# Expert stage of a decoder layer: another order of the half-width gating on VectorE and ScalarE

## The chip, the core and the metric

The kernel runs on one NeuronCore of a Trainium2 chip. The metric is the device time of one execution in microseconds, here the median of three: 2575.46 (2571.65 to 2578.45).

The engines: TensorE (PE) multiplies matrices, VectorE (DVE) and ScalarE (ACT) work on tiles element by element, GpSimd (POOL) gathers rows, SyncE (SP) issues the weight transfers. Each runs its own list of instructions in order and waits at semaphores for the others.

## The reference

One decoder layer on 1024 tokens of width 1024: attention and a convolution side by side, a mixture of experts, and a gated per-layer embedding, with RMSNorm between. The change touches the experts alone:

```python
# 1024 tokens, each sent to 4 of 32 experts; rows are grouped by expert
gu   = rows @ w_gate_up[e] + b_gate_up[e]            # 1024 -> 2 * 1024
gate = minimum(gu[:, :D_FF], 7.0)
up   = clip(gu[:, D_FF:], -7.0, 7.0)
hid  = (up + 1.0) * (gate * sigmoid(gate * 1.702))
out  = hid @ w_down[e] + b_down[e]                   # 1024 -> 1024
y    = sum over a token's 4 experts, weighted by its gates
```

## The kernel before

Three stages follow one another: attention and routing (to about 740 us), the experts (to about 2405), and the rest of the layer.

The expert stage works through a list of *items*. An item is up to 128 rows of one expert; where an expert has 1 to 32 rows more than that, the item carries them along as a *tail* in plain fp32. With these inputs there are 38 items, 8 with a tail. An item reads the expert's weights in 12 *pieces* of 1 MB: pieces 0 to 3 are the gate and up columns of the first half of the hidden width (half 0), 4 to 7 those of half 1, 8 to 11 the down projection. A piece passes through four hands:

- SP issues its transfer into one of 6 slots of `raw` as soon as the slot's last piece has been split (L500 to L506, `expert_piece`; in `slot_free` it waits for `lo_ready`);
- ACT rounds it: `whi` = the piece in fp32r (L1734, `split_hi`), 6 slots, up to 6 pieces ahead of PE;
- DVE takes the remainder: `wlo` = `raw` - `whi` (L868, `split_lo`), 4 slots, up to 4 pieces ahead;
- PE multiplies three times for each 128 rows and 512 columns (L609 to L611, `three`): `whi` by the rows' rounded part, `whi` by their remainder, `wlo` by the rounded part. That is 12 matmuls of 512 columns a piece, 144 an item. At the end of each piece it raises `w_free`.

Between the pieces stands the gating, once for each half. When the gate columns of piece 3 (or 7) are through, `gate_done` rises; DVE clamps `gat`, ACT takes the sigmoid of `gat` (L1747), DVE multiplies (L883), clamps `upc` (L887) and forms `hid` (L892). PE transposes `hid` (L596, `turn_hidden`): for half 0 behind piece 5, for half 1 behind piece 8. ACT rounds the transpose (`hhi`, L1751), DVE takes the remainder (`hlo`, L897, `hidden`), and piece 8 needs those of half 0, piece 10 those of half 1. A tail has the same steps on small tiles (`gat_t`, `sig_t`, `hid_t`); PE turns its `hid_t` behind pieces 1 and 5 (L684). Tail products (L668, L676) run four pieces ahead, so an item whose successor has a tail does four of them too.

For the next item, PE turns the gathered rows behind piece 8 (L579), and ACT and DVE split them into `xhi` and `xlo` (L873). At the item's end ACT copies the result to `ysb` (L1767) and writes it out.

The order on each engine is written out by hand: each has a `body` with a loop over c = 0 to 11, one turn a piece. In turn c DVE waits for `w_free` of piece c and then takes the remainder of piece c + 4; ACT waits for the same and rounds piece c + 6. What else an engine does stands in front of or behind that, by the `if` lines. ScalarE's activation functions lie in tables, and the compiler puts an `ACT_TABLE_LOAD` in front of an activation where it can't know that the table is there; at the start of the loop's body it can't.

Of the kernel before, what the change touches and what calls it, by code (L numbers as in the profile page):

```python
# [23 lines left out]
ALU = mybir.AluOpType  # L24
ACT = mybir.ActivationFunctionType
# [17 lines left out]
LIMIT = 7.0  # L43
# [7 lines left out]
PIECES = 12  # L51
# [39 lines left out]
def layer(nc, x, p_in, positions, g_mix_pre, w_in, w_dw, b_dw, g_conv_ln, b_conv_ln, w_out, g_mix_post,  # L91
# [3 lines left out]
    with outer:  # L95
# [5 lines left out]
        def sem(name):  # L101
            return outer.enter_context(nc.semaphore(name))
# [3 lines left out]
        def banks(b, n=1):  # L106
            return bank[:, b:b + n, :].rearrange("p b c -> p (b c)")
# [245 lines left out]
        lo_ready = sem("lo_ready")  # L353
        w_free = sem("w_free")
        gate_done = sem("gate_done")
        gu_used = sem("gu_used")
        gat_ready = sem("gat_ready")
        sig_done = sem("sig_done")
# [198 lines left out]
        def gate_base(half):  # L557
            return 0 if half else 2
# [305 lines left out]
        def experts_dve(dve, finish_gates):  # L864

            def split_lo(n, c):
                dve.wait_ge(hi_ready, PIECES * n + c + 1)
                dve.tensor_tensor(wlo[:, c % LO], raw[:, c % RAW], whi[:, c % HI].bitcast(F32),  # L868
                                  ALU.subtract).then_inc(lo_ready, 1)

            def columns(n):
                dve.wait_ge(xhi_ready, n + 1)
                dve.tensor_tensor(xlo[:].rearrange("p k n -> p (k n)"), banks(XT, 2),  # L873
                                  xhi[:].rearrange("p k n -> p (k n)").bitcast(F32),
                                  ALU.subtract).then_inc(xlo_ready, 1)

            def gate_part(n, half):

                dve.wait_ge(gate_done, 2 * n + half + 1)
                dve.wait_ge(hid_ready, 2 * n + half)  # L880
                dve.tensor_scalar(gat[:], banks(gate_base(half)), LIMIT, None, ALU.min).then_inc(gat_ready, 1)  # L881
                dve.wait_ge(sig_done, 2 * n + half + 1)
                dve.tensor_tensor(sig[:], gat[:], sig[:], ALU.mult).then_inc(gs_done, 1)  # L883

            def up_part(n, half):

                dve.tensor_scalar(upc[:], banks(gate_base(half) + 1), LIMIT, -LIMIT, ALU.min, ALU.max).then_inc(gu_used, 1)  # L887
                dve.wait_ge(gs_done, 2 * n + half + 1)
                dve.wait_ge(gu_used, 2 * n + half + 1)

                dve.wait_ge(ht_done, 2 * n + half)
                dve.scalar_tensor_tensor(out=hid[:], in0=upc[:], scalar=1.0, in1=sig[:],  # L892
                                         op0=ALU.add, op1=ALU.mult).then_inc(hid_ready, 1)

            def hidden(n, half):
                dve.wait_ge(hhi_ready, 2 * n + half + 1)
                dve.tensor_tensor(hlo[:, 4 * half:4 * half + 4].rearrange("p k n -> p (k n)"), banks(HT),  # L897
                                  hhi[:, 4 * half:4 * half + 4].rearrange("p k n -> p (k n)").bitcast(F32),
                                  ALU.subtract).then_inc(hlo_ready, 1)

            def tail_first(k1, half, fetched):

                if half == 0:
                    dve.wait_ge(bias_t_in, 64 * fetched)
                dve.wait_ge(tail_free, PIECES * k1 + 4 * half + 4)
                dve.wait_ge(hid_t_ready, 2 * k1 + half)
                dve.tensor_tensor(sums[:].rearrange("p (g n) -> p g n", g=2),
                                  banks(SUM if half else ACC)[:, 0:256].rearrange("p (g n) -> p g n", g=2),
                                  bias_t[:, :, half], ALU.add).then_inc(sums_ready, 1)
                dve.wait_ge(sums_ready, 2 * k1 + half + 1)  # L910
                dve.tensor_scalar(gat_t[:], sums[:, 0:P], LIMIT, None, ALU.min).then_inc(gat_t_ready, 1)
                dve.tensor_scalar(upc_t[:], sums[:, P:2 * P], LIMIT, -LIMIT, ALU.min, ALU.max).then_inc(upc_t_ready, 1)

            def tail_gated(k1, half):
                dve.wait_ge(sig_t_done, 2 * k1 + half + 1)
                dve.tensor_tensor(sig_t[:], gat_t[:], sig_t[:], ALU.mult).then_inc(gs_t_done, 1)
                dve.wait_ge(gs_t_done, 2 * k1 + half + 1)
                dve.wait_ge(upc_t_ready, 2 * k1 + half + 1)

                dve.wait_ge(htt_done, 2 * k1 + half)  # L920
                dve.scalar_tensor_tensor(out=hid_t[:], in0=upc_t[:], scalar=1.0, in1=sig_t[:],
                                         op0=ALU.add, op1=ALU.mult).then_inc(hid_t_ready, 1)

            def tail_rows(k1, fetched):

                dve.wait_ge(tail_free, PIECES * k1 + PIECES)
                dve.wait_ge(bias_d_in, 64 * fetched)
                dve.wait_ge(ytail_out, 64 * k1)
                dve.tensor_tensor(ysb_t[:], banks(ACC)[:, 0:256], bias_d[:], ALU.add).then_inc(ytail_ready, 1)

            for s in range(2):
                dve.wait_ge(u2_out[s], 16 * NT // 2)
            dve.wait_ge(u2t_done, 2 * NT)
            for c in range(LO):
                split_lo(0, c)
                if c == 1:
                    columns(0)
            dve.wait_ge(stage3_end, 4)
            dve.wait_ge(tab_in, 16)
            items = Items(dve, "dve", (LIVE, TWO), True)  # L940
            with dve.If(items.value(TWO) > 0):
                tail_first(0, 0, 1)
            finish_gates()

            def body(n, k1, tail):
                nk1 = k1 + tail
                for c in range(PIECES):
                    if tail and c == 8:
                        tail_rows(k1, items.kf)
                    if tail and c == 5:  # L950
                        tail_gated(k1, 1)
                    if c in (3, 7):
                        gate_part(n, c // 4)
                        dve.wait_ge(w_free, PIECES * n + c + 1)
                        up_part(n, c // 4)
                    if c == 5:
                        items.ahead(n + 1)
                        nxt, nxt2 = items.value(LIVE), items.value(TWO)
                    if c + LO < PIECES:
                        dve.wait_ge(w_free, PIECES * n + c + 1)  # L960
                        split_lo(n, c + LO)
                    else:
                        with dve.If(nxt > 0):
                            if c == 9:
                                columns(n + 1)
                            dve.wait_ge(w_free, PIECES * n + c + 1)
                            split_lo(n + 1, c + LO - PIECES)
                    if c in (5, 8):
                        hidden(n, c // 8)
                    if tail and c == 0:  # L970
                        tail_gated(k1, 0)
                    if tail and c == 4:
                        tail_first(k1, 1, None)
                    if c == 11:
                        with dve.If(nxt2 > 0):
                            tail_first(nk1, 0, items.kf + tail)

            items.run(body)
            dve.memset(gat[:, 0:1], 0.0).then_inc(stage4_end, 1)
            dve.wait_ge(stage4_end, 4)  # L980
# [597 lines left out]
        def _(act):  # L1578
# [166 lines left out]
            def sigmoid(n, half):  # L1745
                act.wait_ge(gat_ready, 2 * n + half + 1)
                act.activation(sig[:], gat[:], ACT.Sigmoid, scale=ALPHA).then_inc(sig_done, 1)  # L1747
# [44 lines left out]
            def body(n, k1, tail):  # L1792
                nk1 = k1 + tail
                for c in range(PIECES):
                    if tail and c in (2, 6):
                        tail_hidden(k1, c // 4)
                    if c == 7:
                        with act.If(nxt2 > 0):
                            tail_columns(nk1)
                    if c in (3, 7):  # L1800
                        sigmoid(n, c // 4)
                    if tail and c == 5:
                        tail_sigmoid(k1, 1)
                    if c in (5, 8):
# [3 lines left out]
                    if c + HI < PIECES:  # L1808
                        act.wait_ge(w_free, PIECES * n + c + 1)
                        split_hi(n, c + HI)  # L1810
                    else:
                        with act.If(nxt > 0):
                            act.wait_ge(w_free, PIECES * n + c + 1)
                            split_hi(n + 1, c + HI - PIECES)
                            if c == 8:
                                columns(n + 1)
                    if tail and c == 0:
                        tail_sigmoid(k1, 0)
                    if c == 8:
# [457 lines left out]
```

## Time and profile before

| | before |
|---|---|
| median of 3 runs | 2575.46 us (2571.65 to 2578.45) |
| profiled execution | 2574.06 us, span 2572.4 |
| PE busy | 2382.9 us (93% of the span) |
| DVE busy | 1811.8 us (70%) |
| ACT busy | 1444.4 us (56%) |
| POOL busy | 258.8 us (10%) |
| weight remainders (L868) | 456 x 2288 ns |
| weight roundings (L1734) | 456 x 1912 ns |
| table loads | 1283 ns each |
| granted TensorE clock, mean | 0.97 of full |
| DMA | 629.50 MB, mean 245 GB/s over the span |

Busy time says how much an engine did, not whether it set the pace: that is read from the waits of the engine that has least room. A granted clock of 1.00 is 2.4 GHz; the other level is 0.5, 1.2 GHz, so a stretch with a mean of 0.96 spent a part of its time at half speed. A matmul's end is modelled, so successive ones overlap in the rows. In a row of the timeline, the brackets give the idle time of the engine before the instruction and what released it.

### The profile page before, as it was taken

Reading aid. Unit: us, or ns where it says so; the run is one execution under the profiler, and the core shown is the slowest. Engines: PE = TensorE matmul, PEld = TensorE weight load, DVE = VectorE, ACT = ScalarE, POOL = GpSimd, SP = SyncE. Lnnn points to the kernel's source line nnn. Section 1 sums busy time; section 2 is a strip of 40 time slices with the busy share of each in tenths; the row PEclk is TensorE's granted clock in tenths of the full one; section 3 lists DMA queues with packets and bytes.
Section 4 is the critical chain, followed back from the end, with each engine's and each line's share of the span. In section 5 each row is a group of like instructions: output and inputs, shape, how many; then the busy total and the mean of one; then the engine's idle time right before and its main releaser. Section 6 shows DMA issues by size and latency. Waiting matters only on the chain. (4 is left out here: it accounts for less than half of the span.)

```text
span 2572.4 us, 39278 instructions
## 1 busy us (share of the span) xinstructions
PE 2382.9 (93%) x11242; PEld 1587.9 (62%) x11243; DVE 1811.8 (70%) x2101; ACT 1444.4 (56%) x1441; POOL 258.8 (10%) x252
## 2 busy tenths in 40 slices
PE   6999999999869999999999999999999999999898
PEld 3454445545537777677677776777676676776543
DVE  4573555535468888778888787888787787887374
ACT  3113344444346777577767766676665675776344
POOL 1200000001220001000000001000111010011130
PEclk9999999999879999999999999999999999999999
DMA  6007800142358999799999999899988797998651
GB/s 190 21 13 261 301 21 22 42 174 74 107 173 293 342 332 343 263 335 326 340 326 332 333 323 331 291 331 325 330 290 273 258 340 266 337 326 286 255 205 57
DMA packets 291339, 629.50 MB, mean 245 GB/s; under 512 B 21634, under 2 KB 69506, under 8 KB 291219
## 3 DMA queue, kind: packets, MB, share of 16 engines
q1 hardware_dynamic: 235538, 532.20, 59.6%
q10 hardware_dynamic: 40304, 55.05, 5.9%
q0 software_dynamic: 15440, 41.51, 4.9%
q8 instruction: 33, 0.54, 0.1%
q14 instruction: 24, 0.19, 0.0%
HBM read 558.55 MB, written 68.57 MB: 244 GB/s over the span
## 5 line engine op out<-in xcount | busy, mean ns | idle before, releaser
L868 DVE TENSOR_TENSOR wlo<-raw,whi 128x2048 fp32r<-128x2048 f32 x456 | 1034.7, 2288 | 173.8 <-PE bank L611 171.8
L1734 ACT ACTIVATE whi<-raw 128x2048 fp32r<-128x2048 f32 x456 | 868.2, 1912 | 291.7 <-PE bank L611 167.6
L609 PE MATMUL bank<-whi,xhi 128*128 128x512 f32 x1216 | 501.1, 412 | 8.8 <-issue 8.5
L611 PE MATMUL bank<-wlo,xhi 128*128 128x512 f32 x1216 | 481.4, 396 | 0.0
L610 PE MATMUL bank<-whi,xlo 128*128 128x512 f32 x1216 | 480.8, 395 | 0.0
L609 PEld LDWEIGHTS bank<-whi,xhi 128*128 128x128 f32 x1216 | 229.1, 188 | 106.8 <-issue 61.0
L611 PEld LDWEIGHTS bank<-wlo,xhi 128*128 128x128 f32 x1216 | 228.8, 188 | 55.1
L609 PE MATMUL bank<-whi,hhi 128*128 128x512 f32 x608 | 254.3, 418 | 5.4 <-DVE hlo L897 5.4
L610 PEld LDWEIGHTS bank<-whi,xlo 128*128 128x128 f32 x1216 | 229.2, 188 | 45.9
L610 PE MATMUL bank<-whi,hlo 128*128 128x512 f32 x608 | 242.0, 398 | 0.0
L611 PE MATMUL bank<-wlo,hhi 128*128 128x512 f32 x608 | 241.1, 396 | 0.0
L609 PEld LDWEIGHTS bank<-whi,hhi 128*128 128x128 f32 x608 | 118.5, 195 | 49.2 <-issue 18.4
L1276 POOL DMA_DIRECT2D ids<-token_list x37 | 20.6, 556 | 1181.9 <-PE bank L579 1127.9
L883 DVE TENSOR_TENSOR sig<-gat,sig 128x512 f32<-128x512 f32 x76 | 52.6, 692 | 116.9 <-ACT sig L1747 116.9
L611 PEld LDWEIGHTS bank<-wlo,hhi 128*128 128x128 f32 x608 | 117.0, 192 | 26.7
L610 PEld LDWEIGHTS bank<-whi,hlo 128*128 128x128 f32 x608 | 118.1, 194 | 21.8
L1948 DVE CUSTOM_DVE_ANT_0 S<-bank,mlog 128x512 f32<-128x512 f32 (+3 forms) x144 | 73.1, 554 | 76.3 <-PE bank L1392 53.0
L1638 ACT ACTIVATE PT<-bank 128x512 f32<-128x512 f32 (+3 forms) x96 | 44.5, 513 | 131.1 <-PE bank L1407 131.1
L772 PE MATMUL bank<-raw,h2T 128*128 128x512 f32 x256 | 111.3, 593 | 1.2 <-ACT h2T L819 1.2
L1747 ACT ACTIVATE sig<-gat 128x512 f32<-128x512 f32 x76 | 48.0, 632 | 109.5 <-DVE gat L881 109.0
L1462 PE MATMUL bank<-uT,xall 128*128 128x512 f32 x224 | 101.7, 597 | 0.7 <-ACT qT L1679 0.7
L596 PE MATMUL bank<-cst,hid 128*128 128x128 f32 x304 | 49.8, 288 | 54.8 <-DVE hid L892 54.8
(295 smaller groups left out, 2924.0 us busy)
## 6 DMA issues: line engine op xcount, KB each, us to landing
raw<-in_w_gate_up_dram SPq DMA_DIRECT2D x608, 512.0 KB, 6.1
raw<-in_w_down_dram SPq DMA_DIRECT2D x152, 1024.0 KB, 10.3
expert_rows<-zeros ACTq DMA_DIRECT2D x1, 33280.0 KB, 105.4
expert_rows<-ysb ACTq DMA_DIRECT2D x38, 512.0 KB, 8.5
xall<-in_x_dram SPq DMA_DIRECT2D x8, 512.0 KB, 11.7
uT<-in_w_out_dram SPq DMA_DIRECT2D x1, 4096.0 KB, 12.8
raw<-in_w_ple_gate_dram SPq DMA_DIRECT2D x1, 4096.0 KB, 20.4
h<-h_scratch SPq DMA_DIRECT2D x8, 512.0 KB, 6.4
```

The source lines that it names most:

```text
L596: mm = pe.transpose(banks(HT)[:, k * P:k * P + P], hid[:, k * P:k * P + P], ident)
L609: pe.matmul(dst, stat_hi[:, kt], hi, start=first, stop=False)
L610: pe.matmul(dst, stat_lo[:, kt], hi, start=False, stop=False)
L611: return pe.matmul(dst, stat_hi[:, kt], lo, start=False, stop=last)
L772: mm = pe.matmul(banks(4 + 2 * (t % 2) + half), h2T[t % 2][:, k], wpg[:, k, half * 512:half * 512 + 512], start=(k == 0), stop=(k == KD - 1))
L868: dve.tensor_tensor(wlo[:, c % LO], raw[:, c % RAW], whi[:, c % HI].bitcast(F32), ALU.subtract).then_inc(lo_ready, 1)
L883: dve.tensor_tensor(sig[:], gat[:], sig[:], ALU.mult).then_inc(gs_done, 1)
L1462: pe.matmul(banks(2 + half), mixT[:, k, t * P:t * P + P], wout[:, k, half * 512:half * 512 + 512], start=(k == 0), stop=False)
L1638: act.activation(PT[:, 0, h, 0:n], banks(4 + h)[:, 0:n], ACT.Copy).then_inc(pt_act, 1)
L1734: act.activation(whi[:, c % HI], raw[:, c % RAW], ACT.Copy).then_inc(hi_ready, 1)
L1747: act.activation(sig[:], gat[:], ACT.Sigmoid, scale=ALPHA).then_inc(sig_done, 1)
L1948: dve.tensor_tensor_reduce(out=S[b][:, c * 512:c * 512 + w], in0=score_bank(s, c, h)[:, 0:w], in1=mlog[:, T - n + c * 512:T - n + c * 512 ...
```

## The change

It touches the bodies of the expert stage on DVE and ACT:

- DVE's gating of a half is cut in two. The first part (`gate_part`) holds both clamps, `gat` and, behind the wait for `w_free`, `upc`. The second (`gated`) waits for the sigmoid, multiplies, and forms `hid`. For half 0 the second part moves from turn 3 to turn 4, so that the remainder of piece 7 stands between the two. For half 1 both stay in turn 7.
- DVE's `hidden(n, 1)` moves in front of the next item's first remainder in turn 8.
- ACT takes half 0's sigmoid behind the rounding of piece 9 in turn 3, no longer in front of it. Half 1's sigmoid stays.
- At the head of turn 0 ACT runs a sigmoid of one column into `mark`, a tile that nothing in the stage reads. A new semaphore `table_set` orders it behind the last one. The compiler's table load goes in front of it.

```diff
@@ DVE
                 dve.tensor_scalar(gat[:], banks(gate_base(half)), LIMIT, None, ALU.min).then_inc(gat_ready, 1)
+                dve.wait_ge(w_free, PIECES * n + 4 * half + 4)
+                dve.tensor_scalar(upc[:], banks(gate_base(half) + 1), LIMIT, -LIMIT, ALU.min, ALU.max).then_inc(gu_used, 1)
+
+            def gated(n, half):
+
                 dve.wait_ge(sig_done, 2 * n + half + 1)
                 dve.tensor_tensor(sig[:], gat[:], sig[:], ALU.mult).then_inc(gs_done, 1)
-
-            def up_part(n, half):
-
-                dve.tensor_scalar(upc[:], banks(gate_base(half) + 1), LIMIT, -LIMIT, ALU.min, ALU.max).then_inc(gu_used, 1)
                 dve.wait_ge(gs_done, 2 * n + half + 1)
...
                     if c in (3, 7):
                         gate_part(n, c // 4)
-                        dve.wait_ge(w_free, PIECES * n + c + 1)
-                        up_part(n, c // 4)
+                    if c in (4, 7):
+                        gated(n, c // 7)
+                    if c == 8:
+                        hidden(n, 1)
...
-                    if c in (5, 8):
-                        hidden(n, c // 8)
+                    if c == 5:
+                        hidden(n, 0)
@@ ACT
-                    if c in (3, 7):
-                        sigmoid(n, c // 4)
+                    if c == 0:
+                        act.wait_ge(table_set, n)
+                        act.activation(mark[:], ident[:, 0:1], ACT.Sigmoid).then_inc(table_set, 1)
+                    if c == 7:
+                        sigmoid(n, 1)
...
+                    if c == 3:
+                        sigmoid(n, 0)
```

The order of DVE in turns 2 to 4 of an item with a tail (the other kind reads the same), before; `gat`, `upc`, `sig` and `hid` are the gating of half 0, `wlo` the remainders of pieces 6, 7 and 8:

```order
L868 TENSOR_TENSOR wlo<-raw,whi 128x2048 [waits hi_ready]
L879 ISA
L881 TENSOR_SCALAR gat<-bank 128x512 [waits hid_ready,gate_done]
L883 TENSOR_TENSOR sig<-gat,sig 128x512 [waits sig_done]
L954 REGISTER_ALU
L887 TENSOR_SCALAR upc<-bank 128x512 [waits w_free]
L892 SCALAR_TENSOR_TENSOR hid<-upc,sig 128x512 [waits ht_done,gu_used,gs_done]
L867 REGISTER_ALU [waits w_free]
L868 TENSOR_TENSOR wlo<-raw,whi 128x2048 [waits hi_ready]
```

The same place now:

```order
L869 TENSOR_TENSOR wlo<-raw,whi 128x2048 [waits hi_ready]
L880 ISA
L882 TENSOR_SCALAR gat<-bank 128x512 [waits hid_ready,gate_done]
L883 REGISTER_ALU
L884 TENSOR_SCALAR upc<-bank 128x512 [waits w_free]
L868 REGISTER_ALU [waits w_free]
L869 TENSOR_TENSOR wlo<-raw,whi 128x2048 [waits hi_ready]
L889 TENSOR_TENSOR sig<-gat,sig 128x512 [waits sig_done]
L894 SCALAR_TENSOR_TENSOR hid<-upc,sig 128x512 [waits ht_done,gu_used,gs_done]
```

The clamp of `upc` and the remainder of piece 7 have moved in front of the wait for the sigmoid.

DVE in turns 7 and 8, before (gating of half 1, the remainders of piece 11 and of the next item's piece 0, and `hlo` of half 1):

```order
L881 TENSOR_SCALAR gat<-bank 128x512 [waits hid_ready,gate_done]
L883 TENSOR_TENSOR sig<-gat,sig 128x512 [waits sig_done]
L887 TENSOR_SCALAR upc<-bank 128x512 [waits w_free]
L892 SCALAR_TENSOR_TENSOR hid<-upc,sig 128x512 [waits ht_done,gu_used,gs_done]
L867 REGISTER_ALU [waits w_free]
L868 TENSOR_TENSOR wlo<-raw,whi 128x2048 [waits hi_ready]
L963 COMPARE_AND_BRANCH
L867 ISA [waits w_free]
L868 TENSOR_TENSOR wlo<-raw,whi 128x2048 [waits hi_ready]
L963 UNCONDITIONAL_BRANCH
L897 TENSOR_TENSOR hlo<-bank,hhi 128x512 [waits hhi_ready]
```

And now:

```order
L882 TENSOR_SCALAR gat<-bank 128x512 [waits hid_ready,gate_done]
L884 TENSOR_SCALAR upc<-bank 128x512 [waits w_free]
L889 TENSOR_TENSOR sig<-gat,sig 128x512 [waits sig_done]
L894 SCALAR_TENSOR_TENSOR hid<-upc,sig 128x512 [waits ht_done,gu_used,gs_done]
L868 REGISTER_ALU [waits w_free]
L869 TENSOR_TENSOR wlo<-raw,whi 128x2048 [waits hi_ready]
L899 TENSOR_TENSOR hlo<-bank,hhi 128x512 [waits hhi_ready]
L967 COMPARE_AND_BRANCH
L868 ISA [waits w_free]
L869 TENSOR_TENSOR wlo<-raw,whi 128x2048 [waits hi_ready]
```

The clamp stands in front of the product, and `hlo` in front of the next item's first remainder.

ACT at the head of an item without a tail, before (`raw_in0` and `raw_in1` are the slots of pieces 6 and 7):

```order
L1809 ISA
L1733 ISA [waits w_free]
L1734 ACT_TABLE_LOAD
L1734 ACTIVATE whi<-raw 128x2048 [waits raw_in0]
L1809 REGISTER_ALU
L1734 ACTIVATE whi<-raw 128x2048 [waits raw_in1,w_free]
```

And now:

```order
L1806 ACT_TABLE_LOAD
L1806 ACTIVATE mark<-cst 128x1 [waits table_set]
L1816 ISA
L1737 ISA [waits w_free]
L1738 ACTIVATE whi<-raw 128x2048 [waits raw_in0]
```

ACT in turns 2 and 3 of the same item, before (slots 2 and 3: pieces 8 and 9):

```order
L1734 ACTIVATE whi<-raw 128x2048 [waits raw_in2]
L1746 ISA
L1747 ACT_TABLE_LOAD
L1747 ACTIVATE sig<-gat 128x512 [waits gat_ready]
L1809 REGISTER_ALU
L1734 ACTIVATE whi<-raw 128x2048 [waits raw_in3,w_free]
```

And now:

```order
L1738 ACTIVATE whi<-raw 128x2048 [waits raw_in2]
L1816 REGISTER_ALU
L1738 ACTIVATE whi<-raw 128x2048 [waits raw_in3,w_free]
L1750 ISA
L1751 ACTIVATE sig<-gat 128x512 [waits gat_ready]
```

One load has gone and the other stands in front of the wait for `w_free`; the sigmoid stands behind the rounding that waits for `raw_in3`.

## Rows read from the trace of the kernel before

**Rows 1.** Stretches: length, busy time of PE, PEld, DVE, ACT, POOL; clock, DMA share, GB/s
```profile
1173.06:1214.38 41.32, 39.01 (x168) 30.41 (x167) 34.39 (x24) 29.48 (x22) 2.21 (x2) 0.96 0.95 334
2268.44:2308.12 39.68, 37.75 (x168) 28.76 (x167) 34.32 (x24) 29.36 (x23) 5.25 (x4) 1.00 0.94 336
745.00:2404.50 1659.50, 1566.47 (x7826) 1154.63 (x7814) 1323.87 (x960) 1116.90 (x829) 133.23 (x143) 0.98 0.89 311
```

**Rows 2.** Timeline of ACT: start, length, instruction; first and last `ysb` of an item
```profile
789.68 0.57 ACT L1767 ACTIVATE ysb<-bank 128x512 f32<-128x512 f32 x1
...
2403.25 0.60 ACT L1767 ACTIVATE ysb<-bank 128x512 f32<-128x512 f32 x1 [6.31 <-PE bank L611]
```

**Rows 3.** Timeline of PE, the item from 2268 to 2308
```profile
2298.03 0.66 PE L596 MATMUL bank<-cst,hid 128*128 128x128 f32 x4 [1.27 <-DVE hid L892]
...
2303.13 0.47 PE L609 MATMUL bank<-whi,hhi 128*128 128x512 f32 x1 [0.66 <-DVE hlo L897]
```

**Rows 4.** Waits of PE: who waited for whom, us in total, times, longest
```profile
PE bank L596 <- DVE hid L892: 54.8, 30, 2.1
...
PE bank L684 <- DVE hid_t L921: 15.1, 8, 1.9
```

**Rows 5.** Groups by line: the expert stage's table loads; busy us, mean ns, idle before
```profile
L1734 ACT ACT_TABLE_LOAD x38 | 48.8, 1283 | 37.4 <-PE bank L611 37.4
...
L1747 ACT ACT_TABLE_LOAD x30 | 38.5, 1283 | 0.5
...
L1756 ACT ACT_TABLE_LOAD x8 | 10.3, 1283 | 0.1
```

**Rows 6.** Timeline of PE, the item from 1173 to 1214
```profile
1191.89 0.60 PE L596 MATMUL bank<-cst,hid 128*128 128x128 f32 x4
...
1201.17 0.39 PE L610 MATMUL bank<-whi,hlo 128*128 128x512 f32 x1
1201.40 0.39 PE L611 MATMUL bank<-wlo,hhi 128*128 128x512 f32 x1
1203.86 1.11 PE L596 MATMUL bank<-cst,hid 128*128 128x128 f32 x4 [2.07 <-DVE hid L892]
```

**Rows 7.** Timeline of ACT, the same item, half 0
```profile
1186.98 1.28 ACT L1747 ACT_TABLE_LOAD   x1
1188.27 0.64 ACT L1747 ACTIVATE sig<-gat 128x512 f32<-128x512 f32 x1
```

**Rows 8.** Timeline of DVE, the same item
```profile
1188.94 0.69 DVE L883 TENSOR_TENSOR sig<-gat,sig 128x512 f32<-128x512 f32 x1 [2.88 <-ACT sig L1747]
...
1190.33 0.69 DVE L892 SCALAR_TENSOR_TENSOR hid<-upc,sig 128x512 f32<-128x512 f32 x1
...
1200.34 0.68 DVE L881 TENSOR_SCALAR gat<-bank 128x512 f32<-128x512 f32 x1
1201.72 0.69 DVE L883 TENSOR_TENSOR sig<-gat,sig 128x512 f32<-128x512 f32 x1 [0.70 <-ACT sig L1747]
...
1203.11 0.69 DVE L892 SCALAR_TENSOR_TENSOR hid<-upc,sig 128x512 f32<-128x512 f32 x1
1203.72 4.49 DVE L868 TENSOR_TENSOR wlo<-raw,whi 128x2048 fp32r<-128x2048 f32 x2
```

**Rows 9.** Timelines of ACT and PE, start of the tail item from 1039
```profile
1045.18 1.28 ACT L1734 ACT_TABLE_LOAD   x1 [1.57 <-PE bank L611]
...
1050.96 0.30 PE L684 MATMUL bank<-cst,hid_t 128*128 128x128 f32 x1 [1.89 <-DVE hid_t L921]
```

**Rows 10.** SP's issue of piece 9, KB and us to landing, then DMA 1180 to 1193
```profile
1176.63 0.37 SPq L506 DMA_DIRECT2D raw<-in_w_down_dram  x1
...
raw<-in_w_down_dram SPq DMA_DIRECT2D x1, 1024.0 KB, 11.0
...
DMA packets 1591, 5.35 MB, mean 412 GB/s; under 512 B 107, under 2 KB 107, under 8 KB 1591
```

**Rows 11.** Timeline of ACT, the item from 2308, piece 9
```profile
2324.91 1.92 ACT L1734 ACTIVATE whi<-raw 128x2048 fp32r<-128x2048 f32 x1 [0.39 <-DMA raw<-in_w_down_dram]
```

More of the change, by code:

```diff
@@ L355, in layer @@
         gate_done = sem("gate_done")
+        table_set = sem("table_set")
         gu_used = sem("gu_used")
```

## The prediction

> **What bounds the kernel now.** PE is by far the busiest engine on the page, so I cut the span by stage. In the expert stage, the only part that the diff touches, PE is busy 1566 of 1659.5 us, DVE 1324, ACT 1117, and the transfers look nearly full too (share 0.89) [rows 1]. A busy PE may still be waited on, so I asked what makes an item longer than PE's work. The starts of `ysb` mark the ends of the 38 items: first 789.68, last 2403.25 [rows 2]. Of the 37 periods between them, 24 belong to items without a tail and without one next, mean 41.28 us; 6 to items that already feed the next one's tail, mean 43.33; 7 to tail items, mean 51.84 (sum 1613.5). In the fastest plain item, of 39.68 us, PE waited twice, 1.27 us for `hid` and 0.66 for `hlo` [rows 1, 3]. Matmul records are drawn 0.39 long while the next starts after 0.23 [rows 6], so each wait is truly 0.16 longer: PE's own work is 39.68 - 1.43 - 0.82 = 37.43 us. The other plain items are 3.85 us longer than that on average, and the waits say why: PE waited 54.8 us in 30 waits (one per item without a tail) for `hid`, and 15.1 us in 8 waits for `hid_t` [rows 4]. Behind the long waits PE also loses clock: the item from 1173 to 1214 has a granted clock of 0.96 with a wait of 2.07 in it, the one with a wait of 1.27 has 1.00 [rows 1, 3, 6]. So the bound is PE with one stall per item. The transfers have reserve: while many are queued they move 412 GB/s, against 334 over the item [rows 1, 10].
>
> **The change, part by part**, in the item that begins at 1173 (pieces 0 to 11; 0 to 7 gate and up, 8 to 11 down).
>
> *One table load instead of two.* ACT has 38 + 30 + 8 loads of 1283 ns, two per item [rows 5]. After, one stands at the item's head, in front of the wait for PE. In a plain item the second load (1186.98) delayed the half-0 sigmoid by 1.28 us [rows 7]. In a tail item a load of 1.28 goes from between `whi` and `sig_t`, and the other moves to idle time: at 1045.18 ACT had sat idle 1.57 us for PE [rows 9], which holds a load of 1.28 and the tiny activation behind it. So `sig_t` comes 2 x 1.28 = 2.56 us earlier, more than the 1.89 us that PE waited in this item [rows 9], and the whole wait goes: 15.1 + 8 x 0.16 = 16.4 us saved. What is late next there is PE itself.
>
> The Trainium skill (ScalarE: Activation LUTs, What ACT_TABLE_LOAD costs) adds a drain of about 1.38 us to each switch. The trace disagrees: the sigmoid starts 1.29 us behind the load's start [rows 7]. By the page an item's saving on ACT would be 2.66 us, which would still end no later on PE, so I go by the row.
>
> *Half 0: DVE no longer waits for the sigmoid.* Before, the product came at 1188.94 after 2.88 us idle, `hid` at 1190.33 [rows 8], then the remainders 7, 8, 9. After, `upc` and remainder 7 stand between, so this idle is mostly filled, and remainder 7 no longer stands behind `hid`. For the path that gives: from half 0's `hid` to half 1's `gat` DVE had 1200.34 - 1190.33 = 10.01 us of unbroken work; one remainder leaves it, 4.49 for two and a little overlap, so 2.2: 7.81 [rows 8].
>
> *Half 1: clamp before the product.* Before, `gat` 1200.34, product 1201.72, `hid` 1203.11, PE 1203.86: 3.52 us [rows 6, 8]. Product to `hid` was 1.39 with `upc` between; now `upc` stands beside the sigmoid, and `hid` follows when the product is through (0.69 and some 0.08): 1.38 + 0.77 + 0.75 = 2.90. So PE can turn half 1 at `hid`0 + 7.81 + 2.90 = `hid`0 + 10.71. PE itself is at the end of piece 8 at 1201.40 + 0.23 = 1201.63, from its turn at 1191.89 that is 9.74 [rows 6], less about 0.24 waited for `hlo` of half 0, which now also comes 2.2 us earlier relative to its `hid`: 9.50. It started that turn 0.75 behind `hid`0 at the earliest, so it is there at `hid`0 + 10.25 when half 0 has held it. Left of the wait: 0.46 us, 24 times. In the 6 feeding items more work stands before; I take none.
>
> *Inner remainder first.* `hidden(n, 1)` goes ahead of remainder 0 of the next item. PE waited 0.66 for it before piece 10 in the fast item [rows 3]; after, it is ready 2.2 us earlier. Cost: remainders 0, 1, 2 of the next item one short operation later, covered by three pieces of PE's work; this cover is gone only if DVE is full, and it is busy 34.39 of 41.32 us [rows 1]: 88% of the period I arrive at.
>
> *Half 0: sigmoid behind the rounding.* The one part that adds a wait. ACT now takes `whi` 9 first, and that waits for its transfer; behind it stand the sigmoid, DVE's product, `hid`, remainders 8 to 10, and PE's turn in front of piece 6. Piece 9 was issued at 1176.63 and landed 11.0 us later, at 1187.6 [rows 10]. From there: start 0.05, `whi` 1.92, sigmoid to product 1188.94 - 1188.27 = 0.67, product to `hid` 0.77, to PE 0.75 [rows 7, 8, 11]: 4.16, so 1191.8. PE turned at 1191.89. With the landing of before there is no stall, by 0.1 us. But the transfers move. The chain on DVE from half 1's `hid` to the next item's remainders is fixed, while PE reaches the next item sooner: at full clock its end mark stands 2308.12 - 2298.03 - 0.82 = 9.3 behind the turn [rows 1, 3], 10.0 behind `hid`1; in this item it was 1214.38 - 1203.11 = 11.3. Remainder 0 of the next item, which frees the slot of its piece 6, ended 6.2 us before the mark (1203.72 + 4.49, [rows 8]) and would end at `hid`1 + 5.8 (`hid` itself, two remainders and the inner one), 4.2 before: 2.0 later in that count. The slots of pieces 7 to 9 follow at PE's pace and are less late, so I take 1.3 for the landing of piece 9: stall 1.2. Bounds: 0, the landing of before, which is the nearest row; and, from an item where `whi` 9 itself waited for its transfer (2324.91, 16.8 behind that item's start mark at 2308.12, against 14.5 here) [rows 1, 11], 2.3 later, a stall of 2.2.
>
> **Sum.** Plain items: 37.43 + 0.46 + 1.2 = 39.09 against 41.28, 24 x -2.19 = -53. Feeding items: a wait of 54.8 / 30 + 0.16 = 2.0 goes, 1.2 comes, 6 x -0.8 = -5. Tail items -16; a stall before piece 6 I take as nothing there, since the same bytes have 51.8 us. Clock: waits up to 1.4 us left the full clock (the 39.68 us item); for a few items with a later landing I add 4 x 1.65 (0.04 of 41.3) = +6. Together -68. The profiled execution took 2574.06 (span 2572.4), so 2506; the median of the three runs is 1.4 higher: 2507.5, forecast 2508.
>
> **The rivals.** A, no new stall: the landing of piece 9 stays where it is. For it: from 1180 to 1193 the queue is full and 412 GB/s flow [rows 10], so later issues need not mean later landings. Against: the start of that rush would be later. Items of 38.1 (0.2 left by late ones), gain 24 x 3.2 + 6 x 1.8 + 16 = 104: 2472. The Trainium skill (DMA: Bandwidth & Descriptors, Anatomy of one DMA) gives 2.0 us + bytes / 436 GB/s, for 1 MB 4.4 us; by that rule piece 9 would land at 1181.0 and A holds with room. The row has 11.0, since others stand before it.
>
> B, slower: the same wait grows. The faster items ask 13.8 MB (334 GB/s x 41.32 us) in 39.1, 353 GB/s; if the transfers can't follow, piece 9 lands later and later, PE stalls before piece 6 in every item, and goes on at half clock. Zero gain needs 30 x = 24 x 3.39 + 6 x 2.0 + 16 = 109, x = 3.6 us per item; with half of the items paying 1.65 for the clock that is a stall of 2.8, a landing 2.9 us later than now. From there on the kernel is slower. At 4.0 later: items of 42.6, +32 + 16 - 16 = +32: 2607. Against: the 412 GB/s.
>
> C, between: 2.1 us of stall and half clock in every second item (the late row): items of 40.9, 24 x -0.4 + 6 x 1.0 - 16 = -20: 2555.
>
> D, nothing changes: PE's wait for `hid` at half 1 stays, because DVE comes late from the longer chain (it would be full). Tail saving alone, 2559; against it are the 6.9 us that DVE is idle in the item [rows 1].
>
> **How the numbers follow.** Forecast 0.55, A 0.18, C 0.11, D 0.03, B 0.06, and 0.07 that gains and losses cancel within 0.3% (7.7 us, about what a measurement here tells from nothing). Faster: 0.55 + 0.18 + 0.11 + 0.03 = 0.87; same 0.07; slower 0.06. The likeliest case's own range is 2485 to 2530; the full one reaches to A and close to C, 2470 to 2552.
>
> **What would show it.** Right: 38 table loads fewer; the wait for `hid_t` gone; the wait for `hid` at half 1 under 0.6 us each, and a new wait for `hid` in front of piece 6 of about 1 us with DVE's product waiting for the sigmoid and `whi` 9 for its transfer; period of plain items 38 to 40; granted clock nearer 1.00. Wrong: periods above 41 with `whi` 9 waiting for its transfer over 3 us (B), or DVE without idle time (D).

## The result and the profile after

| | before | after |
|---|---|---|
| median of the runs beside each other | 2576.95 us (2571.65 to 2579.78, 4 runs) | 2498.69 us (2495.82 to 2502.80, 4 runs) |
| ratio, 95% interval | | 0.970 (0.968 to 0.972) |
| span of the profiled execution | 2572.4 us | 2501.1 us |
| mean period, 24 plain items | 41.28 us | 38.83 us |
| mean period, 6 feeding items | 43.33 us | 44.52 us |
| mean period, 7 tail items | 51.84 us | 49.56 us |

The changed kernel is 78 us faster; the forecast was 2508, 68 less than before. The spans differ by 71.3 us, and the 37 periods account for 24 x 2.45 + 7 x 2.28 - 6 x 1.19 = 67.6 of them; 3 of the rest lie before the end of the first item, which has a tail too. (The medians differ by 78 and the spans by 71.3 because the profiled execution of the changed kernel was the longest of its four, 2502.80 us.) The feeding items became slower on average, through two of the six, of 47.07 and 47.34 us; the other four average 43.18, the six before 43.33.

The stretches of a plain item, of a feeding item and of the stage, with the columns of [rows 1]:

```profile
1154.00:1193.00 39.00, 37.78 (x168) 28.84 (x167) 34.22 (x24) 28.46 (x22) 3.53 (x3) 1.00 0.97 351
1504.20:1551.30 47.10, 42.98 (x222) 31.23 (x221) 35.72 (x24) 28.88 (x23) 7.62 (x12) 0.96 0.96 331
745.00:2333.00 1588.00, 1540.92 (x7803) 1134.24 (x7802) 1317.27 (x955) 1074.48 (x825) 122.53 (x143) 0.99 0.92 325
```

The stage fell from 1659.5 to 1588 us, PE's clock in it rose from 0.98 to 0.99. Items in which the clock fell to its lower level went from 17 to 4. The waits of PE, against [rows 4], and the table loads, against [rows 5] (ACT, both from the views by line):

```profile
PE bank L597 <- DVE hid L894: 34.1, 47, 4.1
...
PE bank L685 <- DVE hid_t L923: 1.7, 1, 1.7
```

```profile
L1806 ACT ACT_TABLE_LOAD x38 | 48.8, 1283 | 0.8 <-issue 0.2
L1751 ACT ACTIVATE sig<-gat 128x512 f32<-128x512 f32 x76 | 47.3, 622 | 62.2 <-DVE gat L882 62.2
```

The 38 loads left stand at the items' heads. One `hid_t` wait of eight is left. The wait for `hid` shrank from 54.8 to 34.1 us, but it now occurs 47 times: it has split in two. Taken from the gaps between the starts of PE's matmuls, and so 0.16 us longer each than the waits in the rows, the mean of the plain items is: half 1 had 2.08 us and has 0.37; half 0 had none and has 0.74. All waits "per plain item" below are taken in this way.

The item from 1153.78, half 0. First ACT, then DVE, then PE:

```profile
1169.73 1.92 ACT L1738 ACTIVATE whi<-raw 128x2048 fp32r<-128x2048 f32 x1 [0.70 <-DMA raw<-in_w_down_dram]
1171.55 0.61 ACT L1751 ACTIVATE sig<-gat 128x512 f32<-128x512 f32 x1
```

```profile
1166.09 0.68 DVE L882 TENSOR_SCALAR gat<-bank 128x512 f32<-128x512 f32 x1
1166.69 0.68 DVE L884 TENSOR_SCALAR upc<-bank 128x512 f32<-128x512 f32 x1
1167.29 2.28 DVE L869 TENSOR_TENSOR wlo<-raw,whi 128x2048 fp32r<-128x2048 f32 x1
1172.20 0.69 DVE L889 TENSOR_TENSOR sig<-gat,sig 128x512 f32<-128x512 f32 x1 [2.63 <-ACT sig L1751]
1172.92 0.69 DVE L894 SCALAR_TENSOR_TENSOR hid<-upc,sig 128x512 f32<-128x512 f32 x1
...
1182.85 0.69 DVE L894 SCALAR_TENSOR_TENSOR hid<-upc,sig 128x512 f32<-128x512 f32 x1
```

```profile
1173.67 0.66 PE L597 MATMUL bank<-cst,hid 128*128 128x128 f32 x4 [0.89 <-DVE hid L894]
...
1183.59 0.66 PE L597 MATMUL bank<-cst,hid 128*128 128x128 f32 x4 [0.33 <-DVE hid L894]
```

`whi` 9 waits for its transfer until 1169.73, the sigmoid stands behind it though `gat` was there since 1166.8, DVE is idle 2.63 us, and PE waits 0.89 in front of piece 6. From the landing to PE's turn it is 1173.67 - 1169.68 = 3.99 us; the prediction had 4.16. `hid` to `hid` is 9.93 us, where [rows 8] had 12.78; the wait left at half 1 is 0.33.

A feeding item has the same chain with a later landing (ACT, DVE, PE of the item from 1504.2):

```profile
1523.20 1.91 ACT L1738 ACTIVATE whi<-raw 128x2048 fp32r<-128x2048 f32 x1 [3.63 <-DMA raw<-in_w_down_dram]
```

```profile
1525.66 0.69 DVE L889 TENSOR_TENSOR sig<-gat,sig 128x512 f32<-128x512 f32 x1 [5.85 <-ACT sig L1751]
```

```profile
1527.14 0.66 PE L597 MATMUL bank<-cst,hid 128*128 128x128 f32 x4 [4.12 <-DVE hid L894]
```

Piece 9 took 15.2 us from issue to landing there, against 12.0 in the plain item. The transfers of the last stretch before the two landings, 1517.5 to 1523.2 and then 1165 to 1169.7:

```profile
DMA packets 527, 1.58 MB, mean 277 GB/s; under 512 B 124, under 2 KB 124, under 8 KB 527
...
q0 software_dynamic: 237, 0.46, 29.9%
```

```profile
DMA packets 515, 1.96 MB, mean 417 GB/s; under 512 B 37, under 2 KB 37, under 8 KB 515
...
q0 software_dynamic: 5, 0.01, 0.5%
```

GpSimd's queue (q0) has the tail's bias and row transfers in it there, and the whole moves 277 GB/s instead of 417. The landings of pieces 8 and 9 say the same for all six feeding items: where no packet of q0 lies between the two (two items), they are 2.56 us apart, as in the plain items; with 102 packets it is 3.96 us, with 156 4.90, with 206 5.57 and with 229, in the item shown, 5.49.

A tail item's head, ACT from 1029.98 and PE's turn of `hid_t`, against [rows 9]:

```profile
1029.98 1.92 ACT L1738 ACTIVATE whi<-raw 128x2048 fp32r<-128x2048 f32 x1 [0.70 <-ACT ysb L1771]
1031.92 1.28 ACT L1806 ACT_TABLE_LOAD   x1
1033.21 0.20 ACT L1806 ACTIVATE mark<-cst 128x1 f32<-128x1 f32 x1
1033.47 1.92 ACT L1738 ACTIVATE whi<-raw 128x2048 fp32r<-128x2048 f32 x1
1035.29 0.29 ACT L1760 ACTIVATE sig_t<-gat_t 128x128 f32<-128x128 f32 x1
```

```profile
1037.19 0.27 PE L685 MATMUL bank<-cst,hid_t 128*128 128x128 f32 x1
```

No load stands between `whi` and `sig_t` any more, and PE finds `hid_t` ready.

### The profile page after: what moved, and what is told of

It reads as the page before. It is cut to its first block, busy times and chain, and to the rows that moved or that the text cites. A ratio compares the mean times of both kernels' runs of the same rounds, so it can differ in the third digit from the quotient of the medians.

```text
span 2501.1 us, 39278 instructions
## 1 busy us (share of the span) xinstructions
PE 2358.1 (94%) x11242; PEld 1569.2 (63%) x11243; DVE 1807.6 (72%) x2101; ACT 1405.2 (56%) x1441; POOL 248.6 (10%) x252
## 4 chain that ended last, share of the span: by engine, by line
PE 56%; DVE 17%; DMA 14%; issue 7%; ACT 2%; DVEq 2%; SPq 1%; POOL 0%; ACTq 0%; POOLq 0%
DMA raw<-in_w_down_dram 11%; DVE wlo L869 11%; PE bank L610 8%; PE bank L612 7%; PE bank L611 7%; PE bank L1353 6%; PE bank L773 4%; PE bank L1466 4%; PE bank L1376 3%; PE bank L669 3%; PE bank L1343 2%; PE bank L1396 2%; PE bank L1425 2%; PE bank L1411 2%; DVE sig L889 1%
## 5 line engine op out<-in xcount | busy, mean ns | idle before, releaser
L610 PE MATMUL bank<-whi,hhi 128*128 128x512 f32 x608 | 246.8, 406 | 0.0
L1353 PE MATMUL bank<-uT,wk 128*128 128x512 f32 x192 | 94.9, 615 | 1.2 <-ACT qraw L1617 1.2
L1353 PE MATMUL bank<-uT,wq 128*128 128x512 f32 x192 | 93.6, 616 | 0.1
```

Of the source, the lines that this page charges most:

```text
L610: pe.matmul(dst, stat_hi[:, kt], hi, start=first, stop=False)
L1353: mm = pe.matmul(banks(bank_no), w[:, k], uT[:, k, half * 512:half * 512 + 512], start=(k == 0), stop=(k == KD - 1))
```

## The experiments

Each was timed against the kernel before on the same chip (three rounds; before: 2574.19 us in the first four, 2581.01 in the next four, 2581.15 in the last). The kernel before was thus 7 us slower beside e5 to e9 than beside e1 to e4; where runs of different groups are compared, the difference by the ratios stands in brackets. Intervals are of the ratio to before; the changed kernel's is 0.968 to 0.972. Periods are means over 24 plain and 6 feeding items of the profiled execution. "Landing" is the time from the item's start mark to the landing of piece 9, the mean of the 24 plain items; before it was 14.58, after 15.50 (feeding: 15.22 and 16.94).

**e1: half 0's sigmoid in front of the rounding of piece 9**, the rest as changed.

```diff
-                    if c == 7:
-                        sigmoid(n, 1)
+                    if c in (3, 7):
+                        sigmoid(n, c // 4)
                     (split_hi of piece c + 6)
-                    if c == 3:
-                        sigmoid(n, 0)
```

> The changed kernel (2498.7 us) with half 0's sigmoid back in front of the rounding of piece 9. Theory (the new wait of PE in front of piece 6 comes from piece 9's landing, through ACT): that wait goes, plain items fall from 38.83 to about 37.5, 24 x 1.3 + 6 x 1 = 37 us less, so about 2462. Rival 1 (the wait is DVE's, which now takes remainder 7 ahead of the product): nothing moves, 2498. Rival 2 (the transfers are the bound once PE has no stall): under 10 us gained, 2490, with ACT's waits for transfers growing by what PE's wait loses.

Measured: 2459.07 us, ratio 0.955 (0.953 to 0.956); plain 37.39, feeding 42.44, landing 14.92 and 15.26. The waits of PE for `hid`, two stretches (an item, the stage), and ACT, DVE, PE at half 0 of the item from 1146.1:

```profile
PE bank L597 <- DVE hid L894: 4.9, 5, 1.3
```

```profile
1146.10:1183.20 37.10, 37.10 (x167) 28.93 (x167) 34.26 (x24) 28.45 (x22) 3.30 (x3) 1.00 0.99 368
745.00:2288.00 1543.00, 1524.67 (x7811) 1134.56 (x7809) 1320.60 (x956) 1075.78 (x827) 137.48 (x143) 1.00 0.93 335
```

```profile
1158.42 1.92 ACT L1738 ACTIVATE whi<-raw 128x2048 fp32r<-128x2048 f32 x1 [3.04 <-DMA raw<-in_w_down_dram]
1160.24 0.61 ACT L1751 ACTIVATE sig<-gat 128x512 f32<-128x512 f32 x1
1161.05 1.92 ACT L1738 ACTIVATE whi<-raw 128x2048 fp32r<-128x2048 f32 x1 [0.19 <-DMA raw<-in_w_down_dram]
```

```profile
1161.70 0.69 DVE L889 TENSOR_TENSOR sig<-gat,sig 128x512 f32<-128x512 f32 x1
1162.41 0.69 DVE L894 SCALAR_TENSOR_TENSOR hid<-upc,sig 128x512 f32<-128x512 f32 x1
```

```profile
1164.82 0.60 PE L597 MATMUL bank<-cst,hid 128*128 128x128 f32 x4
```

The new wait is gone and took 40 us with it. PE is busy without a gap through the item, 37.10 of 37.10 us, at 368 GB/s. The product follows remainder 7 with no idle time: the remainder between the clamps and the product covers the sigmoid. `hid` is there 1.7 us before PE's turn needs it (1164.82 - 0.75 - 1162.41). This is the fastest version that computes everything, and it beats both kernels.

**e2: without the table load at the head**, everything else as changed.

```diff
-                    if c == 0:
-                        act.wait_ge(table_set, n)
-                        act.activation(mark[:], ident[:, 0:1], ACT.Sigmoid).then_inc(table_set, 1)
```

> The changed kernel without the sigmoid of one column at the item's head, so that the compiler places two loads per item as before. Theory (a load in front of the half-0 sigmoid is on the path, the load at the head is hidden): tail items get their wait for hid_t back, 8 x 2.4 = 19, and half 0's hidden rows come 1.28 us later, 30 x 1.28 = 38, so about 2555. Rival (the order of the work made the gain, the load was hidden in the wait for piece 9's transfer): only the tails, about 2517.

Measured: 2557.47 us, 0.993 (0.991 to 0.995); plain 40.33, feeding 44.29, tail 52.28. The table loads of the stage, and PE's waits:

```profile
L1738 ACT ACT_TABLE_LOAD x38 | 48.8, 1283 | 39.7 <-PE bank L612 39.7
L1751 ACT ACT_TABLE_LOAD x30 | 38.5, 1283 | 0.5
...
L1760 ACT ACT_TABLE_LOAD x8 | 10.3, 1283 | 0.1
```

```profile
PE bank L597 <- DVE hid L894: 60.9, 44, 4.8
...
PE bank L685 <- DVE hid_t L923: 15.1, 8, 1.9
```

The second load is back, and with it the wait for `hid_t`, to the tenth as in [rows 4]. In this kernel the load at the head is worth 59 us, three quarters of the gain: in the plain items the second load stands between `whi` 9 and the sigmoid, on the chain that is late. The wait at half 0 grows from 0.74 to 2.00 us per plain item, by one load of 1.28.

**e3: the inner remainder of half 1 late again**, behind remainder 0 of the next item.

```diff
-                    if c == 8:
-                        hidden(n, 1)
...
-                    if c == 5:
-                        hidden(n, 0)
+                    if c in (5, 8):
+                        hidden(n, c // 8)
```

> The changed kernel with hlo of half 1 behind the next item's first remainder again. Theory (PE comes to piece 10 about 14.7 us behind half 0's hidden rows, hlo would be there after 15.6): a wait of about 0.9 before piece 10, 24 x 0.9 = 22, so about 2520. Rival (the remainders of the next item start 0.6 us earlier, so pieces land earlier and the wait before piece 6 shrinks as much): 2500.

Measured: 2497.81 us, 0.970 (0.968 to 0.971): the same as the changed kernel. Plain 39.03, feeding 42.48, landing 14.95. PE's waits, and its piece 10 in the item from 1156.5:

```profile
PE bank L610 <- DVE hlo L899: 13.8, 22, 0.7
PE bank L597 <- DVE hid L894: 12.7, 29, 1.2
```

```profile
1190.14 0.47 PE L610 MATMUL bank<-whi,hhi 128*128 128x512 f32 x1 [0.62 <-DVE hlo L899]
```

My theory lost, the rival won. The wait for `hlo` does come back, 0.62 us, but remainder 0 of the next item is earlier by one short operation, piece 9 lands 0.55 us earlier, and the wait for `hid` falls from 34.1 to 12.7 us. The two cancel, but not in the same items: the plain ones are 0.2 us longer, the feeding ones 2.0 shorter.

**e4: before plus the table load at the head alone.**

```diff
+                    if c == 0:
+                        act.wait_ge(table_set, n)
+                        act.activation(mark[:], ident[:, 0:1], ACT.Sigmoid).then_inc(table_set, 1)
```

> The kernel before (2577) with only the sigmoid of one column at the item's head added, so one table load per item less. Theory (every engine's half-0 chain is 1.28 us earlier, PE's wait for hid of half 1 falls from 2.0 to 0.7, clock losses behind it go, tails save 2.4 each): about 2510, most of the whole gain. Rival (the order made the gain, the load only matters in tails): about 2558.

Measured: 2521.73 us, 0.979 (0.977 to 0.981); plain 40.10, feeding 42.98, tail 49.56; half 1's wait 1.51 per plain item (2.08 before), none at half 0. PE's waits:

```profile
PE bank L597 <- DVE hid L893: 40.8, 30, 2.1
```

52 of the 78 us come from this edit alone; the order of the gating as a whole adds 23. With the sigmoid left in front of the rounding (e1) the order adds 63. The expected 2510 was too low: half 1's wait fell by 0.57 us and not by 1.3. The 1.28 us of the load show as 0.89 in `hid` of half 0 (16.44 us behind the item's start mark on average, before 17.33); piece 8, whose rounding stands in front of the sigmoid, landed 0.34 later there (12.36 against 12.02). A part of what PE gained lies elsewhere, between its two turns, where without the waits at the turns it needs 9.41 us instead of 9.83: its waits in front of piece 8 are shorter.

**e5: no remainder between clamps and product** (half 0's product in turn 3 again), the sigmoid still behind the rounding.

```diff
-                    if c in (4, 7):
-                        gated(n, c // 7)
+                    if c in (3, 7):
+                        gated(n, c // 4)
```

> The changed kernel with half 0's product and hid back in turn 3, so that no weight remainder stands between the clamps and the gating; the sigmoid stays behind the rounding of piece 9. Theory (DVE then idles until piece 9 has landed, been rounded and the sigmoid is through, and remainder 7 comes only behind hid, 2.2 us more between hid of half 0 and gat of half 1): the wait at half 1 grows from 0.45 to 2.7, with clock losses, 30 x 2.2 + 15, so about 2580, no better than before. Rival (DVE has 6 us to spare per item and catches up): 2505.

Measured: 2556.49 us, 0.992 (0.989 to 0.994); plain 40.96, waits 0.77 at half 0 and 1.51 at half 1 per plain item. PE's waits, DVE from the product of the item from 1168.1, and PE's first matmul of piece 8 in it:

```profile
PE bank L597 <- DVE hid L894: 57.1, 53, 1.9
PE bank L604 <- DVE wlo L869: 21.1, 21, 1.0
```

```profile
1186.31 0.69 DVE L889 TENSOR_TENSOR sig<-gat,sig 128x512 f32<-128x512 f32 x1 [4.63 <-ACT sig L1751]
1187.03 0.69 DVE L894 SCALAR_TENSOR_TENSOR hid<-upc,sig 128x512 f32<-128x512 f32 x1
1187.64 6.69 DVE L869 TENSOR_TENSOR wlo<-raw,whi 128x2048 fp32r<-128x2048 f32 x3
1194.25 0.68 DVE L899 TENSOR_TENSOR hlo<-bank,hhi 128x512 fp32r<-128x512 f32 x1
```

```profile
1195.03 0.49 PE L604 MATMUL bank<-bsp,one_r 2*128 2x512 f32 x2 [1.00 <-DVE wlo L869]
```

DVE is idle for all of the sigmoid's lateness, and three remainders in a row (pieces 7, 8 and 9) stand behind `hid`, with `hlo` of half 0 behind them. It costs both: half 1 is late again, and PE has a new wait of 1.0 us in front of piece 8 in 21 items. The view names `wlo` for it, but the third remainder ended at 1194.33 and `hlo`, which piece 8 needs too, at 1194.93, 0.1 us before PE went on: the wait is for `hlo`. The remainder between is worth 58 us (56) where the sigmoid is late. I had expected more, 2580, from a wait of 2.7 us at half 1.

**e6: e1 and e5 together**, that is, against e1:

```diff
-                    if c in (4, 7):
-                        gated(n, c // 7)
+                    if c in (3, 7):
+                        gated(n, c // 4)
```

> The version of e1 (sigmoid in front of piece 9's rounding, 2459) with half 0's product and hid in turn 3, no remainder between. Theory (hid of half 0 comes some 2.3 us earlier, the same work stands between then and gat of half 1, only the 1.3 us until the sigmoid is idle; e1 has under 0.2 us of room at half 1): a wait of 0 to 0.6 in 24 items, 2460 to 2475. Rival (any idle of DVE in turn 3 costs in full, 1.3 x 30): 2498.

Measured: 2488.13 us, 0.965 (0.962 to 0.968), between the theory and the rival; plain 38.42, half 1's wait 0.68 per plain item, none at half 0. Against e1 the remainder between is worth 29 us (26), half of what it is worth behind a late sigmoid. The two edits on half 0 work on the same idle time of DVE.

**e7: half 1's clamp of `upc` behind its product again.** The change: `dve.tensor_scalar(upc ...)` of half 1, with its wait for `w_free`, moves from `gate_part` to `gated`, behind the product.

> The changed kernel with half 1's product in front of the clamp of upc as before. Theory (hid of half 1 comes 0.62 us later and PE has been waiting there in 24 plain items): 24 x 0.62 = 15, about 2514. Rival (PE's later start of the next item lets piece 9 land earlier against it, so the wait before piece 6 shrinks as in e3): 2500.

Measured: 2515.71 us, 0.976 (0.973 to 0.979); plain 39.33, half 1's wait 1.00 per plain item against 0.37. The clamp's 0.6 us is on the path, as expected: 17 us (15).

**e8: half of the down projection's data is not transferred** (the four transfers of 1 MB take only the first of their two parts; the rest of the slot is what stood there, so its output is not the layer's).

```diff
-                sp.dma_start(dst.rearrange("p (k d) n -> p k (d n)", k=2), rows).then_inc(raw_in[slot], 16)
+                sp.dma_start(dst.rearrange("p (k d) n -> p k (d n)", k=2)[:, 0:1], rows[:, 0:1]).then_inc(raw_in[slot], 16)
```

> The changed kernel in which the transfers of the down projection's pieces (8 to 11) bring only the first half of each piece; the other half of the slot keeps what lay there, so this half of the down projection is left out of what is computed; all instructions of PE, ACT and DVE are the same. Theory (the wait before piece 6 is piece 9's landing): it lands 2 us or more earlier, the wait goes although the sigmoid stays behind the rounding, plain items about 37.5, 2462, like e1. Rival (the order on ACT costs it, whatever the transfer does): 2490 or more.

Measured: 2449.71 us, 0.951 (0.948 to 0.953); plain 37.40, feeding 41.19, landing 12.35 (feeding 12.21). ACT at half 0 of the item from 1138.4, with PE's turn:

```profile
1149.55 3.72 ACT L1738 ACTIVATE whi<-raw 128x2048 fp32r<-128x2048 f32 x2 [1.47 <-DMA raw<-in_w_down_dram]
1153.17 0.62 ACT L1751 ACTIVATE sig<-gat 128x512 f32<-128x512 f32 x1
```

```profile
1157.26 0.60 PE L597 MATMUL bank<-cst,hid 128*128 128x128 f32 x4
```

With the same order as the changed kernel and the landing 3.15 us earlier, no wait for `hid` is left in plain and feeding items and the plain period is e1's. So it is the landing, through `whi` 9 and the sigmoid behind it, that holds half 0, and nothing else in the order. That the feeding items are fastest here (41.19) says the same of them.

**e9: e1 with the inner remainder late** (e1's and e3's edits together).

> The changed kernel with both: the sigmoid of half 0 ahead of the rounding of piece 9, and the inner remainder of half 1 behind remainder 0 of the next item. With the order of the sigmoid alone PE had no stall left (plain items 37.4 us, time 2459) so there is no slack that an earlier slot could use. Theory (the inner remainder's two orders trade a wait of PE for an earlier slot, and without a stall before piece 6 the slot is worth nothing): PE waits about 0.5 to 0.65 us for hlo before piece 10 in most of the 24 plain items, periods 37.9 to 38.0, 24 x 0.55 = 13: 2472 us. Rival (DVE catches up by then, since hid comes at 26.9 instead of 28.3 after the mark): no wait, 2459, the same as with the inner remainder first.

Measured: 2467.42 us, 0.956 (0.954 to 0.958); plain 37.81, landing 14.56. In steady items 37.46 against e1's 37.13: 0.33 each, less than the 0.55 expected. The intervals of e1 and e9 overlap, so by the timings the 8 us (2) are not told from nothing; the periods have the theory's sign.

## Why the prediction was right, point by point

**One table load instead of two.** Right in place and mechanism. In the tail items the price was about right: forecast 16.4 us in 8 items (2.05 each), measured 2.28 each, and e4 has 49.56 us per tail item with this edit alone. In the plain items I had counted only what it does on the path; as a share it is the largest part (e4: 52 us), more than I made it look like. The Trainium skill's drain of about 1.38 us per switch (ScalarE: Activation LUTs, What ACT_TABLE_LOAD costs) is not seen here either: the rounding in front ends at 1031.90, the load starts at 1031.92 and the next activation 1.29 us later, at 1033.21. Whether these loads change the set of functions, for which the Trainium skill states the drain, the trace does not say.

**Half 1.** Forecast: 0.46 us left per plain item. Measured 0.37 on average, 0.33 and 0.16 of drawing in the item shown. e7 confirms the clamp's part, e5 and e6 the remainder's.

**Inner remainder first.** This step failed, inside a sum that held. I took the 0.66 us in front of piece 10 as gained and the later remainders as covered by PE's work. They are covered for PE, not for the slots: remainder 0 frees a slot, and landings of piece 9 are 0.55 us later for it (e3) or 0.36 (e1 against e9). With the late sigmoid this gives all back; with the early one 0.3 us per item may remain.

**Half 0, sigmoid behind the rounding.** The chain was right, from landing to PE's turn 3.99 us against 4.16. The term was mis-sized in both directions. Plain items: landing 0.92 later instead of 1.3, wait 0.74 instead of 1.2. Feeding items: landing 1.7 later, wait 2.12 on average and up to 4.28, in items of 47 us; I had forecast -0.8 per item and got +1.19, 12 us in all. What the landing of 15.50 is made of can be read from four runs: 14.56 with neither edit (e9), 14.92 with the inner remainder first (e1), 14.95 with the late sigmoid (e3), 15.50 with both. This fits a wait that feeds itself, since DVE's remainders 8 and 9 stand behind the late product and free the slots of later transfers; no run tests that alone, and e6, without a wait at half 0, has a landing of 15.37 too. Why a landing moves is seen in the issues, counted from the mark: piece 9 itself was issued only 0.23 us later than before (3.80 against 3.57), but pieces 6, 7 and 8 were 0.93, 1.00 and 0.66 later, and piece 9 spent 11.70 us behind them instead of 11.02. The prediction had remainder 0 2.0 us later and guessed 1.3 for the landing.

**Rivals.** A (no new stall) is what the profile of e1 shows, not this order. B (the transfers can't follow) is refuted for plain items: e1 and its 37.10 us ran at 368 GB/s, with the landing earlier than in the slower changed kernel. C (a stall of 2.1 us and half clock in every second item) asked too much: the stall was 0.74 and the clock fell in 4 items of the stage. D (half 1's wait stays) is refuted by its 0.37 us. By the rule of 2.0 us + bytes / 436 GB/s (the Trainium skill, DMA: Bandwidth & Descriptors, Anatomy of one DMA, fitted to transfers that GpSimd issues) 1 MB would take an estimated 4.4 us; piece 9, issued by SP, took 12.0. The difference is what stands in front of it: pieces 8 and 9 land 2.56 us apart, and with half the bytes in the pieces of the down projection piece 9 lands 3.15 us earlier (e8).

**Sum.** Forecast -53 - 5 - 16 + 6 = -68. Measured on the same terms: plain -59 (clock within), feeding +7, tails -16 and about -3 in the first item: -71. With the clock's +6 counted among the plain items they were forecast at -47, so they came out 12 us better and the feeding items 12 us worse: that these two cancelled is luck, and the sum is better than its terms. In the plain items PE's own work is 37.1 us, not 37.43, and both waits were shorter than forecast. Against that stood terms that the sum did not have: the second item of the stage, of 43.27 us (41.20 before), and 0.2 us from PE's turn at half 1 to the mark wherever it had waited (9.12 us, in e1 8.90).

The feeding items' landing moved by 1.7 us and not by 0.9. Of this, 1.0 is there at the landing of piece 8 already (11.79 before, 12.77 after), as in the plain items (12.02 and 12.94). The other 0.7 arises between the landings of pieces 8 and 9, 3.43 us apart before and 4.17 after, and goes with q0's packets in between: 77, 119 and 200 in three of the six items before, 102 to 229 in four after; in e1 two items have any, and in e9 one, with mean landings of 15.26 and 14.97.

What stays open: why the transfers of GpSimd fall into that stretch more often in the changed order; they are in all versions, and in e3, with the inner remainder late, the landing is 15.33 and the feeding period 42.48. The second item of the stage has a wait of PE of 3.92 us that is put down to issue in the changed kernel (2.13 before); I have not tried what it is.

## What to carry to other kernels

An activation behind a rounding that waits for a transfer inherits the transfer's lateness; put the short operation that others wait for in front of the long one that waits for data, and give the waiting engine a piece of its own work between. A short operation moved forward is only free if nothing that it displaces frees a buffer: look for who refills it. And where a compiler reloads an activation table in every turn of a loop, one tiny activation at the head, in idle time, can be worth more than the reordering around it.

## What the runs showed of the hardware

- The DMA engines' busy share says little of the bytes: the feeding item from 1504 has a share of 0.96 at 331 GB/s, the item of e1 0.99 at 368. In the last 5.7 us before the late landing the rate was 277 GB/s with 124 packets under 512 bytes, against 417 with 37 in 4.7 us of the plain item.
- SP's pieces of 1 MB land 2.56 us apart (8 to 9) when GpSimd's queue sends nothing in between, and 5.5 us apart with 206 to 229 packets of that queue between them.
- More bytes per microsecond did not go with later landings: 351 GB/s over an item of the changed kernel and 15.50 us, 368 in e1 and 14.92 (before: 334 and 14.58).
- PE's clock fell to its lower level (1.2 GHz) in 17 items before, 4 after, 1 in e1; that one, the second item of the stage, is among the 4. In the changed kernel waits of up to 1.9 us in front of piece 6 left the full clock; one of 2.1, and those of 3.5 and 4.3 in feeding items, went with the lower one. The length of a wait alone does not decide it: before, 22 waits at half 1 measured 2.00 to 2.25 us from the starts (the 2.07 of [rows 6] is one, of 2.22), of which 16 went with the lower level and 6 left the full clock, in e4 one of 2.24 left it and one of 2.00 did not, and in e2 one of 3.15 left it.
